# A three-block float32 network on one core: opening loads by single k-tiles, shorter warm-up products, and two moves in the fourth mixer

## What is computed

```python
def swiglu(x, wi, wo):
    gate, up = jnp.split(x @ wi, 2, axis=-1)
    return (jax.nn.silu(gate) * up) @ wo

# last mixer, per head
logits = jnp.einsum('bhqd,bhkd->bhqk', q_blk, k) * scale      # + decay, causal mask
probs = jax.nn.softmax(logits, axis=-1)
out = jnp.einsum('bhqk,bhkd->bhqd', probs, v)
k_r = apply_rotary(rms_norm_2(k_rope, k_rope_gain), cos, sin)  # one key part, shared by all 8 heads
k_full = jnp.concatenate([k_nope, k_r], axis=-1)
```

## Time and profile before

| | us |
|---|---|
| median of 3 runs | 1462.19 (1462.1 to 1462.27) |
| profiled execution, own time | 1462.28 |
| its span in the profile | 1460.4 |
| busy PE / PE weight loads / DVE / ACT / POOL | 1453.4 / 1250.2 / 1002.1 / 778.5 / 87.7 |

### The profile page before, as it was taken

How to read it: one execution, slowest core, us unless ns; L and a number is a source line. 1 busy time by engine, 2 the same in 40 slices (tenths; PEclk the granted TensorE clock), 3 DMA queues, 4 the chain that set the end, 5 groups by cost and what they waited for, 6 DMA issues and landing times.

```text
span 1460.4 us, 18625 instructions
## 1 busy us (share of the span) xinstructions
PE 1453.4 (100%) x7822; PEld 1250.2 (86%) x7822; DVE 1002.1 (69%) x1215; ACT 778.5 (53%) x970; POOL 87.7 (6%) x113
## 2 busy tenths in 40 slices
PE   9999999999999999999999999999999999999999
PEld 7888888888888888888888888888888888888887
DVE  6876466777755867459877664787645987687653
ACT  6654355655534555345655543564535876465542
POOL 0000003000000000006100000000000800000000
PEclk9999999999999999999999999999999999999999
DMA  9855563556556555545455555465556543566552
GB/s 328 276 183 178 160 203 116 166 182 201 178 183 201 188 187 188 186 139 172 147 194 195 182 178 201 160 218 186 187 171 218 188 144 117 173 195 202 180 186 72
DMA packets 205620, 266.82 MB, mean 183 GB/s; under 512 B 6944, under 2 KB 148880, under 8 KB 205280
## 3 DMA queue, kind: packets, MB, share of 16 engines
q1 hardware_dynamic: 204320, 261.23, 54.2%
q0 software_dynamic: 1072, 4.35, 0.8%
q10 hardware_dynamic: 144, 0.05, 0.0%
HBM read 264.56 MB, written 1.05 MB: 182 GB/s over the span
## 4 chain that ended last, share of the span: by engine, by line
PE 96%; DVE 2%; ACT 1%; DMA 0%; issue 0%; SPq 0%; ACTq 0%; DVEq 0%
PE ps L635 33%; PE ps L641 17%; PE ps L561 13%; PE ps L563 13%; PE ps L562 13%; PE ps L614 1%; PE ps L715 1%; PE ps L808 1%; DVE wlo L1628 1%; PE ps L748 1%; DMA X<-in_x_turned 0%; DVE d_i L2044 0%; PE ps L749 0%; ACT whi L1189 0%; DVE d_i L2020 0%; PE ps L734 0%
## 5 line engine op out<-in xcount | busy, mean ns | idle before, releaser
L1628 DVE TENSOR_TENSOR wlo<-raw,whi 128x2048 fp32r<-128x2048 f32 (+3 forms) x274 | 567.8, 2077 | 257.3 <-ACT whi L1189 256.9
L1189 ACT CAST whi<-raw 128x2048 fp32r<-128x2048 f32 (+3 forms) x274 | 474.8, 1738 | 222.0 <-PE ps L563 218.1
L635 PE MATMUL ps<-xt,whi 128*128 128x512 f32 x2112 | 511.2, 391 | 0.8 <-DVE xt L2221 0.8
L635 PEld LDWEIGHTS ps<-xt,whi 128*128 128x128 f32 x2112 | 386.1, 188 | 74.8 <-DVE xt L2221 1.8
L641 PEld LDWEIGHTS ps<-xt,wlo 128*128 128x128 f32 x2112 | 274.0, 191 | 12.3
L641 PE MATMUL ps<-xt,wlo 128*128 128x256 f32 x2112 | 277.7, 283 | 0.0
L561 PE MATMUL ps<-whi,xt 128*128 128x512 f32 (+4 forms) x304 | 112.8, 371 | 0.2 <-DVE xt L1642 0.2
L563 PE MATMUL ps<-whi,xt 128*128 128x512 f32 (+4 forms) x304 | 109.7, 361 | 0.0
L562 PE MATMUL ps<-wlo,xt 128*128 128x512 f32 (+4 forms) x304 | 109.5, 360 | 0.0
L561 PEld LDWEIGHTS ps<-whi,xt 128*128 128x128 f32 x304 | 57.3, 189 | 9.6 <-issue 0.7
L563 PEld LDWEIGHTS ps<-whi,xt 128*128 128x128 f32 x304 | 57.2, 188 | 8.5
(11 more groups left out here) (422 smaller groups left out, 1884.9 us busy)
## 6 DMA issues: line engine op xcount, KB each, us to landing
raw<-in_ffn_wi SPq DMA_DIRECT2D x85, 1024.0 KB, 5.0
raw<-in_ffn_wo SPq DMA_DIRECT2D x40, 1024.0 KB, 5.0
raw<-in_ffn_w_gate SPq DMA_DIRECT2D x22, 1024.0 KB, 5.1
raw<-in_ffn_w_up SPq DMA_DIRECT2D x22, 1024.0 KB, 5.1
raw<-in_ffn_w_down SPq DMA_DIRECT2D x20, 1024.0 KB, 4.9
raw<-in_w_in SPq DMA_DIRECT2D x14, 1024.0 KB, 5.1
raw<-in_even_w_in SPq DMA_DIRECT2D x6, 1024.0 KB, 5.3
raw<-in_ffn_wo SPq DMA_DIRECT2D x8, 512.0 KB, 3.8
```

The lines of the kernel that those rows point to most:

```text
L635: return e.matmul(pair.ap[:, b, :], whi[:, v % SPLIT, 256 * j + 128 * b:256 * j + 128 * b + 128], XS[:, j, :, :].rearrange("p h t -> p (h ...
L1189: e.copy(whi[0:n, v % SPLIT, c], raw[0:n, v % RAW, c]).then_inc(s_hi.mark(*[(v, j) for j in js]), 1)
L1628: e.tensor_tensor(wlo[0:n, v % SPLIT, c], raw[0:n, v % RAW, c], whi[0:n, v % SPLIT, c].bitcast(F32), ALU.subtract).then_inc(s_lo.mark(*[(v ...
```

## The change

It has four parts.

1. The opening pieces of x and of the first weight block are loaded, rounded and split as k-tile 0, k-tile 1, k-tiles 2 and 3, and so on (`FIRST`), where they were pairs. There are two more DMAs on SyncE's list, ahead of x for k-tiles 2 and 3, and one more cast on ACT and on DVE.
2. The three warm-up products are 256 wide, not 512.
3. In the last mixer DVE does `logits` of tile 1 of ("f", 0) ahead of the block's splitting, and that of tile 0 after it.
4. PE's `rope_key_turn` moves from behind the first k-tile of g2.2 to behind `probabilities` of ("f", 1), and ACT's copy of it moves ahead of two `unit()` and of the copy of the fox values ("f", 1).

```diff
@@ -21,6 +21,7 @@
 OUTSIDE = -1.0e38
 PICKED = -3.0e38
 WARM = 3
+FIRST = [(0,), (1,), (2, 3), (4, 5), (6, 7)]
 LEVELS = [1, 2, 4, 8, 16, 32, 64]
 
 
@@ -290,7 +291,8 @@
             job, i = plan[v]
             nk, wd = job.blocks[i][1], job.width
             if v < 3:
-                return [((j, j + 1), 128, slice(j * wd, (j + 2) * wd)) for j in range(0, nk, 2)]
+                parts = FIRST if v == 0 else [(0, 1), (2, 3), (4, 5), (6, 7)]
+                return [(js, 128, slice(js[0] * wd, (js[-1] + 1) * wd)) for js in parts]
             if isinstance(job.blocks[i][2], tuple):
                 return [((j,), job.rows(i, j), slice(j * wd, (j + 1) * wd)) for j in range(nk)]
             if job in (a2.u[0], b2.u[0], c2.u[0]):
@@ -299,7 +301,10 @@
 
         def first(v, j):
 
-            return s_first[j // 2 if v == 0 else 2 + 2 * v + j // 4][v, j // (4 if v else 2)]
+            if v == 0:
+                i = next(i for i, js in enumerate(FIRST) if j in js)
+                return s_first[i][0, i]
+            return s_first[3 + 2 * v + j // 4][v, j // 4]
 
         pair_of = {}
 
@@ -488,27 +493,27 @@
             def load_x(i, a, b):
                 e.dma_start(XR[:, a:b, :], turned[:, a:b, :]).then_inc(s_xt[i].mark("x"), 16)
 
-            def load_pair(p):
+            def load_first(i):
                 c0, n = plan[0][0].cols[0]
-                src = plan[0][0].w[256 * p:256 * p + 256, c0:c0 + n].rearrange("(k p) n -> p k n", p=128)
-                e.dma_start(raw[:, 0, 512 * p:512 * p + 512].rearrange("p (k n) -> p k n", k=2), src).then_inc(s_first[p].mark((0, p)), 16)
-
-            load_x(0, 0, 2)
-            load_pair(0)
-            load_x(1, 2, 4)
-            load_pair(1)
+                a, b = FIRST[i][0], FIRST[i][-1] + 1
+                src = plan[0][0].w[128 * a:128 * b, c0:c0 + n].rearrange("(k p) n -> p k n", p=128)
+                e.dma_start(raw[:, 0, 256 * a:256 * b].rearrange("p (k n) -> p k n", k=b - a), src).then_inc(s_first[i].mark((0, i)), 16)
+
+            for i, (a, b) in enumerate(((0, 1), (1, 2), (2, 4))):
+                load_x(i, a, b)
+                load_first(i)
 
             def load_half(v, h):
                 c0, n = plan[v][0].cols[0]
                 slot = raw[:, v, 1024 * h:1024 * h + 1024].rearrange("p (k n) -> p k n", k=4)
                 src = plan[v][0].w[512 * h:512 * h + 512, c0:c0 + n].rearrange("(k p) n -> p k n", p=128)
-                e.dma_start(slot, src).then_inc(s_first[2 + 2 * v + h].mark((v, h)), 16)
+                e.dma_start(slot, src).then_inc(s_first[3 + 2 * v + h].mark((v, h)), 16)
 
             load_half(1, 0)
             load_half(2, 0)
-            load_x(2, 4, 8)
-            load_pair(2)
-            load_pair(3)
+            load_x(3, 4, 8)
+            load_first(3)
+            load_first(4)
             load_half(1, 1)
             load_half(2, 1)
             e.dma_start(ident[:, :], T["c_ident"]).then_inc(s_const.mark("all"), 16)
@@ -1099,12 +1104,12 @@
                 fox_values(0)
                 steps(gate2[1], 1, 0, 2)
                 probabilities(mat, ("f", 1), 1)
+                rope_key_turn()
                 steps(gate2[1], 1, 2, 3)
                 fox_values(1)
                 steps(gate2[1], 1, 3)
                 give(gate2[1].name, s_dve["gate", 1])
                 steps(gate2[2], 0, 0, 1)
-                rope_key_turn()
                 mla_queries(0)
                 mla_keys()
                 steps(gate2[2], 0, 1, 3)
@@ -1158,7 +1163,7 @@
             warm = take("warm")
             q.wait_ge(*s_dve["warm"])
             for i in range(WARM):
-                t = warm_up(512)
+                t = warm_up(256)
             t.then_inc(s_turn.mark("warm"), 1)
             give("warm", s_turn["warm"])
             ffn(a1)
@@ -1537,12 +1543,12 @@
                 unit()
                 turned(("m_", "v", ("f", 0)), YT, 4, None, (128,) * 2)
                 probabilities(mat, ("f", 1), ("f", 0))
-                unit()
-                turned(("m_", "v", ("f", 1)), YT, 6, None, (128,) * 2)
-                unit()
                 q.wait_ge(*s_turn["m_", "s", ("f", 1), 0])
                 q.wait_ge(*s_turn["krt"])
                 e.copy(mKT[64:96, :, :], bc(Pair("krt").ap[64:96, 0, 0:256], 1, 8)).then_inc(s_act.mark("krt"), 1)
+                unit()
+                turned(("m_", "v", ("f", 1)), YT, 6, None, (128,) * 2)
+                unit()
                 mla_queries(0)
                 mla_keys(0)
                 mla_keys(1)
@@ -1582,15 +1588,13 @@
             def x_high(j):
 
                 q.wait_ge(*s_gain0["all"])
-                q.wait_ge(*s_xt[min(j // 2, 2)]["x"])
+                q.wait_ge(*s_xt[(0, 1, 2, 2, 3, 3, 3, 3)[j]]["x"])
                 e.mul(XT.hi[:, j, :], XR[:, j, :], gain("f1", j)).then_inc(s_act.mark(("x0", j)), 1)
 
-            x_high(0)
-            x_high(1)
-            high(0, *pieces(0)[0])
-            x_high(2)
-            x_high(3)
-            high(0, *pieces(0)[1])
+            for i in range(3):
+                for j in FIRST[i]:
+                    x_high(j)
+                high(0, *pieces(0)[i])
             half(1, 0)
             half(2, 0)
             ffn(a1)
@@ -2149,8 +2154,9 @@
                 head_factors("q")
                 unit()
                 head_scale("q")
-                unit()
-                logits(mat, ("f", 0), 0, causal)
+                logits(mat, ("f", 0), 0, causal, None, (1,))
+                unit()
+                logits(mat, ("f", 0), 0, causal, None, (0,))
                 logits(mat, ("f", 1), 1, causal, ("fxk", 1))
                 normalise(mat, ("f", 0), 0)
                 unit()
@@ -2221,12 +2227,10 @@
                 e.scalar_tensor_tensor(XT.lo[:, j, :], XR[:, j, :], gain("f1", j), XT.hi[:, j, :].bitcast(F32),
                                        ALU.mult, ALU.subtract).then_inc(s_dve.mark((("xt", "in"), j)), 1)
 
-            x_low(0)
-            x_low(1)
-            low(0, *pieces(0)[0], done=False)
-            x_low(2)
-            x_low(3)
-            low(0, *pieces(0)[1], done=False)
+            for i in range(3):
+                for j in FIRST[i]:
+                    x_low(j)
+                low(0, *pieces(0)[i], done=False)
             half(1, 0)
             half(2, 0)
             ffn(a1)
```

More of the change, by code:

```diff
@@ L201, in program @@
         s_raw = [signal(f"s_raw{i}", 16) for i in range(RAW)]
-        s_first = [signal(f"s_first{j}", 16) for j in range(8)]
-        s_xt = [signal(f"s_xt{j}", 16) for j in range(3)]
+        s_first = [signal(f"s_first{j}", 16) for j in range(9)]
+        s_xt = [signal(f"s_xt{j}", 16) for j in range(4)]
         s_x = signal("s_x", 16)
@@ L1257, in ffn @@
                         x_high(j)
-                    half(0, 1)
+                    for p in pieces(0)[3:]:
+                        high(0, *p)
                     half(1, 1)
@@ L1539, in mla @@
                 probabilities(mat, ("f", 1), ("f", 0))
+                q.wait_ge(*s_turn["m_", "s", ("f", 1), 0])
+                q.wait_ge(*s_turn["krt"])
+                e.copy(mKT[64:96, :, :], bc(Pair("krt").ap[64:96, 0, 0:256], 1, 8)).then_inc(s_act.mark("krt"), 1)
                 unit()
@@ L1542, in mla @@
                 unit()
-                q.wait_ge(*s_turn["m_", "s", ("f", 1), 0])
-                q.wait_ge(*s_turn["krt"])
-                e.copy(mKT[64:96, :, :], bc(Pair("krt").ap[64:96, 0, 0:256], 1, 8)).then_inc(s_act.mark("krt"), 1)
                 mla_queries(0)
@@ L1731, in ffn @@
                         x_low(j)
-                    half(0, 1)
+                    for p in pieces(0)[3:]:
+                        low(0, *p, done=p[0][-1] == 7)
                     half(1, 1)
```

## The result

The changed kernel takes **1465.33 us** (median of 15 runs, 1463.15 to 1466.54) against 1462.13 (15 runs, 1461.8 to 1462.32): +3.2 us, a ratio of 1.0021 with a 95% interval from 1.0013 to 1.0028. It is slower, where no change was forecast (1462.5, range 1461.0 to 1464.0). The scatter has grown too, from 0.5 us to 3.4. The profiled execution took 1465.82 us, its span is 1463.9, 3.5 more than before.

What follows compares the result with a forecast made beforehand. TensorE, busy 96% of the span, bounds the kernel, so only its standstills can give time. Opening +0.15, warm-up 0, logits +0.48, keys -0.36 make +0.27 on 1462.28, or 1462.55; the median lies 0.09 lower: 1462.5, range 1461.0 to 1464.0.

Steps and rivals of the forecast that it cites:

- I take 0 and keep the failure as a rival: Opening: warm-up products half as wide cost nothing if TensorE's clock is at its upper level by then; 0 us.
- the rival with the right mechanism: Opening: warm-up ends before TensorE's clock rises, so first products run slow; 1463.4 us, long form 1465.2; chance 0.18.
- The later pieces are issued later too ... and I cost them at nothing: Opening: loads behind x of k-tiles 2 and 3 are issued 0.90 us later, but TensorE has no gap there; 0.
- The bytes ahead are the same 512 KB ... so I take a value near the lower half, +0.15: Opening: x of k-tiles 2 and 3, issued 0.90 us later, lands between 0.2 us sooner and 0.9 later; +0.15 us.
- The first product: Opening: TensorE starts at about 6.05 us instead of 6.54, worth nothing since it then waits for k-tile 2.
- The last mixer: Last mixer: first logits by halves cost +0.48 us, turned keys sooner give -0.36 us.
- the late split: Last mixer: VectorE's block splitting ends at 1175.65 us instead of 1175.02, holding TensorE's next block; +0.48 us.
- the clock: Rival, opening: clock still low after the shorter warm-up, first products take twice as long; 1463.4 or 1465.2 us; chance 0.18.
- the late transfer: Rival, opening: x of k-tiles 2 and 3 pays its later issue whole, +0.9 for +0.15; 1463.2 us; chance 0.10.
- The two short forms: Opening rivals: x of k-tiles 2 and 3 late by +0.9 (chance 0.10); clock low for only 3.4 us more, 1463.4.
- The transfer of x is late in full: Rival, opening: x of k-tiles 2 and 3 costs +0.9 us instead of +0.15; 1463.2 us; chance 0.10.
- The mixer gives what it promises: Rival, last mixer: both TensorE waits vanish whole, -0.94 and -0.36, with opening at best, -0.2; 1460.8 us; chance 0.10.

Runs made afterwards that it cites:

- the version above: Kernel before with turned keys sooner, three gate-block splittings halved (one half ahead of the first fox logits), fox values' low parts moved: 1460.76 us against 1462.06.

## Why the prediction was wrong

- **"I take 0 and keep the failure as a rival"** (the shorter warm-up). This step failed: a term was put at nothing that costs 1.1 us by itself and 1.8 on top of the new opening. The short warm-up ended at 4.39 us. The rows for it had been read the earlier trace rows: the clock rose after the shorter warm-up would have ended. That was evidence for the loss, and the rival with the right mechanism got a chance of 0.18. The nearness of the two moments was no reason against it, and their distance came from one trace: of the eleven kernels here with the long warm-up, three have its last weight load, near 4.9 us, at the full pace (0.19 us), and in eight the one at 5.04 us still takes 0.28 to 0.34.
- **"The later pieces are issued later too ... and I cost them at nothing"** (the opening). This step failed too, and it is why the loads alone cost 1.25 us where +0.15 was taken. In the two traces with the new loads and the long warm-up the weights of k-tiles 2 and 3 head the chain, issued 1.0 to 1.1 us later and landed 1.3 to 1.6 us later than before, and k-tile 2 starts 1.32 and 1.57 us late. That TensorE had no gap after 8.35 us said nothing about these weights, since k-tile 2 itself waits for them.
- **"The bytes ahead are the same 512 KB ... so I take a value near the lower half, +0.15"** (x itself). The issue came at 2.60 us as forecast (2.55). In those two traces the transfer took 5.0 us, inside the bounds of 4.0 and 5.11 but at the upper one, so x landed 0.8 us late: the value within the bounds was chosen wrongly. In the changed kernel's own trace it took 6.36 us, outside them. The upper bound was taken from transfers cut as before, so it did not bound the changed ones. The section of the Trainium skill that the prediction names here for a fixed cost of about 2 us describes DMAs issued by GpSimd; these are issued by SyncE, and no run here isolates such a cost.
- **The first product** came at 4.73 us, not 6.05: the gains landed 0.75 + 2.9 = 3.65 us into the run instead of at 4.98. That early start is worth nothing, as the prediction said; the kernel with single casts alone shows it (first product at 5.95 us, 0.0 gained).
- **The last mixer** came out as worked out, to 0.1 us at each point: VectorE's lost 0.63 us (0.56 shown as idle), the second scores' gain of 0.94 eaten by the pair's logits and then by the late split, +0.48 (0.56 measured), and -0.36 for the keys (-0.43).
- **The range** (1461.0 to 1464.0) took the clock and the late transfer as alternatives. They came together, and the measured 1465.33 is beyond it. The two short forms added to the forecast, +0.9 and +0.75, would have given 1464.1, outside the range already. The chance of slower, 0.04, was too small for the same reason.
- Of the rivals, the clock is right in its mechanism (1463.4 forecast, 1463.15 with the short warm-up alone). "The transfer of x is late in full" has x right, 0.8 us late, but the weights behind it set the time: 1463.2 against 1463.55 for the change with the long warm-up. "The mixer gives what it promises" is wrong for the change; that the version above comes out at its 1460.8 is in part luck: the rival takes 1.5 us, 0.2 of them for an opening that the version does not touch, from the profiled execution's 1462.28, and the version takes 1.30 from 1462.06. By the Trainium skill ("TensorE: Matmul & The Clock Gate", "Part 1: The HAM clock gate") the low level is the default until activity lifts it; the runs with three short and with six short products agree, at 1463.15 and 1462.02.

What stays open: why cut pieces lower the rate from 4 to 7 us (192 for 290 GB/s), how much of the loss is the later place in the queue, and whether the shorter warm-up makes x land later with the new opening or the 0.87 us between two traces are scatter.

## What to carry to other kernels

A warm-up has to run past the moment at which the rows show the clock rising, and that moment should be read from more than one trace; here the one that ended at 4.39 us was too short and those that ended at 5.9 us or later were not. A wider scatter of the runs is a sign of a miss. Cutting the first loads smaller brings only the pieces at the front sooner: look at all the loads that the next k-tile waits for, x and weights, and not only at the one that heads the chain before the change. Where a step is moved ahead because its consumer waits, ask whether its own input is there by then; if not, fill the gap with half of the work that it passed.

## What had not been expected of the hardware

The record of the granted clock reads 1.00 in stretches in which products take twice their pace (four in 2.05 us against 1.17), so it has to be checked against durations at the start of a run. In seven of the fifteen executions of that kernel its mean did fall, to 0.998 or 0.999. With three short warm-up products and the loads of before the runs of one kernel differ by 2.9 us, with three long ones by 0.5 to 1.1 in a set and with six short ones by 0.45. And while the later loads slow down with the cut pieces, a small one on another queue got faster: the gains, 49 KB, landed 2.9 to 3.2 us after their issue with both cut and 3.8 to 4.3 with the pairs.
